# A decoder trunk on one core: the second head's flips moved behind the attention products, four loads given homes of their own or moved, and the bias copies cut in six

## The reference, cut to what matters

```python
# layer 0
rkv = einsum('cbsd,cde->cbse', x_mix[:3], w_rkv)          # receptance, key, value
w = -softplus(-(w0 + tanh(xw @ w1) @ w2)) - 0.5            # decay
a = sigmoid(a0 + (xa @ a1) @ a2)
g = sigmoid(xg @ g1) @ g2                                  # output gate
y = rwkv7_scan(r, decay, k, v, -kk, kk * a)                # 16 heads of 64
out = ((norm(y) + bonus) * g) @ w_o
# layer 1, 16 heads, three groups of (window, dilation)
q, k = rms_norm(q) * scale, rms_norm(k)
logits = q k^T + bias(table, distance)                     # banded
out_g, lse_g = softmax(logits) v, logsumexp(logits)
o = sum_g softmax_g(lse_g) * out_g;  x = x + o @ w_o
# each layer
x = x + (silu(gate) * up) @ w_out
```

## Time and profile before

| what | value |
|---|---|
| median of three runs | 1908.83 us |
| the profiled execution, its own time | 1911.89 us |
| its span, first to last instruction | 1910.1 us |
| mean granted clock of TensorE | 0.983 of full |
| PE busy | 1822.3 us, 95% |
| DVE, ACT, POOL busy | 916.8, 771.9, 194.0 us |
| chain that ended last | PE 67%, ACT 4%, issue 1%, DVE 1% |
| transfers | 155.01 MB, mean 81 GB/s |

### The profile page before, as it was taken

The page is one execution under the profiler, slowest core; times in us unless marked ns, Lnnn a source line. Parts: engine busy times, 40 slices in busy tenths (PEclk is TensorE's granted clock), DMA queues, the critical chain, the costliest instruction groups (busy, mean ns, idle before and its releaser), DMA issues.

```text
span 1910.1 us, 36221 instructions
## 1 busy us (share of the span) xinstructions
PE 1822.3 (95%) x15618; PEld 1382.3 (72%) x15618; DVE 916.8 (48%) x1561; ACT 771.9 (40%) x1310; POOL 194.0 (10%) x172
## 2 busy tenths in 40 slices
PE   8988999988999999999999999999999799999999
PEld 3745655555558888888887777777777688888887
DVE  6624555555444444433454654654654454444322
ACT  4333444443233222222456655655665532222211
POOL 0022333333000000000011111111111000000000
PEclk9988999998999999999999999999999899999999
DMA  3271011102013332333322222222222123333322
GB/s 115 84 249 47 28 31 30 31 28 83 28 55 111 94 98 95 100 99 100 99 78 78 78 67 80 81 63 87 78 67 67 45 90 100 98 100 100 99 93 95
DMA packets 57542, 155.01 MB, mean 81 GB/s; under 512 B 5591, under 2 KB 22535, under 8 KB 57384
## 3 DMA queue, kind: packets, MB, share of 16 engines
q1 hardware_dynamic: 57288, 152.63, 25.4%
q10 hardware_dynamic: 96, 0.07, 0.0%
HBM read 150.51 MB, written 11.61 MB: 85 GB/s over the span
## 4 chain that ended last, share of the span: by engine, by line
PE 67%; ACT 4%; issue 1%; DVE 1%; ACTq 0%; DVEq 0%
PE bank L520 65%; PE bank L523 2%; ACT f L1500 2%; ACT f L1513 1%; ACT f L1487 0%; ACT r L1478 0%; ACT f L1474 0%; DVE r L1861 0%; ACT f L1505 0%; DVE f L1584 0%; ACT r L1194 0%; DVE r L1573 0%; DVE f L1989 0%; ACT L1454 0%; DVE r L2006 0%
## 5 line engine op out<-in xcount | busy, mean ns | idle before, releaser
L520 PE MATMUL bank<-r 128*128 128x512 f32 x5424 | 1262.0, 392 | 6.9 <-DVE r L2006 3.7
L520 PEld LDWEIGHTS bank<-r 128*128 128x128 f32 x5424 | 1013.3, 188 | 234.6 <-issue 19.8
L520 PE MATMUL bank<-f 64*64 64x64 f32 (+5 forms) x9762 | 522.5, 260 | 56.9 <-ACT f L1266 15.6
L520 PEld LDWEIGHTS bank<-f 64*64 64x64 f32 (+3 forms) x9762 | 320.8, 144 | 245.9 <-issue 125.3
L1573 DVE TENSOR_TENSOR r<-f,r 128x1024 fp32r<-128x1024 f32 x222 | 273.2, 1231 | 385.3 <-ACT r L1194 385.3
L1194 ACT ACTIVATE r<-f 128x1024 fp32r<-128x1024 f32 x222 | 232.5, 1048 | 158.4 <-PE bank L520 141.2
L2158 POOL TENSOR_TENSOR r<-f,r 128x512 fp32r<-128x512 f32 x48 | 62.2, 1297 | 862.2 <-ACT r L1478 862.2
L1457 ACT ACTIVATE r<-f 128x512 fp32r<-128x512 f32 x44 | 27.8, 632 | 215.6 <-DVE f L1900 215.6
L1930 DVE TENSOR_TENSOR f<-bank,f 128x512 f32<-128x512 f32 x72 | 56.0, 778 | 87.7 <-PE bank L520 84.4
L1704 DVE TENSOR_TENSOR f<-bank,f 64x512 f32<-64x512 f32 x80 | 55.1, 689 | 65.7 <-PE bank L520 64.4
L523 PE MATMUL bank<-f 128*128 128x128 f32 x432 | 64.8, 280 | 20.8 <-ACT f L1513 14.2
(11 more groups left out here) (106 smaller groups left out, 927.8 us busy)
## 6 DMA issues: line engine op xcount, KB each, us to landing
f<-stream SPq DMA_DIRECT2D x245, 512.0 KB, 3.5
bias_copies<-bias_rows SPq DMA_DIRECT2D x3, 3072.0 KB, 24.4
f<-xT SPq DMA_DIRECT2D x16, 256.0 KB, 4.7
f<-lora_out SPq DMA_DIRECT2D x16, 128.0 KB, 3.8
f<-bias_copies SPq DMA_DIRECT2D x16, 128.0 KB, 3.2
f<-bias_copies SPq DMA_DIRECT2D x32, 64.0 KB, 3.0
outT<-f SPq DMA_DIRECT2D x8, 256.0 KB, 4.2
f<-wo_last SPq DMA_DIRECT2D x2, 512.0 KB, 6.0
```

The source lines that it names most:

```text
L520: return nc.tensor.matmul(out, lhsT, rhs, start=start, stop=stop, skip_group_check=True)
```

## The change

- Panel 11 (tile `PAN_WA`) goes to a home of its own, `O_TG`, and no longer through the raw buffer; SP issues it without a wait, and panel 13 waits only for the split of panel 9. `raw_in` counts the raw buffer's loads accordingly.
- At tile 11 ACT loads the sigmoid table set ahead of its wait, takes the Copy before the Tanh, and splits panel 13 after both.
- The gate and output-gate weights of pairs 0 and 1 get homes in the receptance mix's area and are loaded after tile 10, between panels 13 and 14.
- The three bias copies become six of half the size, one behind the panels of each of k = 0 to 5.
- In the attention stage PE's order in a slot becomes product, aux, first head's flip, logits or attend, second head's flip. ACT's becomes split, drain of head 0, aux, drain of head 1, squares; in slot 5 the split comes behind the drain of head 0.

```diff
@@ homes
-O_LWA = O_CM + N_CM
-O_LWG = O_LWA + 2 * 2 * P
-O_AR = O_LWG + 2 * 2 * P
+O_AR = O_CM + N_CM
...
-O_EP = O_CC + S
+O_LWA = O_CC + S
+O_LWG = O_LWA + 2 * 2 * P
+O_EP = O_LWG + 2 * 2 * P
+assert O_XM <= O_LWA and O_EP <= O_XM + KC * S
@@ 
+        def raw_in(eng, p):
+            early = p > PAN_WA and (p - PAN_WA) % RAW == 0
+            eng.wait_ge(s[f"w_raw{p % RAW}"], 16 * (p // RAW + 1 - early))
@@ SP
             def panel(p):
-                if p >= RAW and is_split(p - RAW):
-                    sp.wait_ge(s["w_lo"], split_of(p - RAW) + 1)
-                elif p >= RAW:
-                    sp.wait_ge(s["dense"], PANEL_AT[p - RAW])
+                held = p - RAW - (RAW if p - RAW == PAN_WA else 0)
+                if p == PAN_WA:
+                    sp.dma_start(f(O_TG, 1024), stream[p]).then_inc(s["w_wa"], 16)
+                    return
+                if held >= 0 and is_split(held):
+                    sp.wait_ge(s["w_lo"], split_of(held) + 1)
+                elif held >= 0:
+                    sp.wait_ge(s["dense"], PANEL_AT[held])
                 sp.dma_start(f(O_RAW + p % RAW * 1024, 1024), stream[p]).then_inc(...)
             for p in range(PAN_PROJ + RAW):
+                if p == PAN_PROJ:
+                    full(sp, PAN_WA - 1)
+                    for hp in range(2):
+                        gate_weights(hp)
+                        output_gate_weights(hp)
                 panel(p)
...
-            gate_weights(0) ... output_gate_weights(1)
-            sp.wait_ge(s["bias_dma"], 48)
-            for g in range(3):        # 16 rows each
-                sp.dma_start(copies ...).then_inc(s["bias_rep"], 16)
+            def copy_bias(n):         # 8 rows each
+                sp.dma_start(copies ...).then_inc(s["bias_rep"], 16)
             for k in range(-1, NHP - 1):
                 if k + 3 < NHP:
                     gate_weights(k + 3)
                 for p in (PAN_PROJ + 2 * (k + 2), PAN_PROJ + 2 * (k + 2) + 1):
                     if p < PAN_WO0 + RAW:
                         panel(p)
+                if 0 <= k < 6:
+                    if k == 0:
+                        sp.wait_ge(s["bias_dma"], 48)
+                    copy_bias(k)
@@ PE, decay_and_gate
-                pe.wait_ge(s[f"w_raw{t % RAW}"], 16 * (t // RAW + 1))
+                pe.wait_ge(s["w_wa"], 16)
-                    w = O_RAW + t % RAW * 1024 + c * P
+                    w = O_TG + c * P
@@ PE, attention
-                    if a >= 0 and 3 <= i <= 6:
-                        flip_probs(a, 0, i - 3)
                     if i and it < NHP:
                         projection_aux(it, i - 1)
...
                     if 3 <= i <= 6:
-                        flip_probs(a, 1, i - 3)
+                        flip_probs(a, 0, i - 3)
                     if i < 4:
                         logits(a, i)
                     if 4 <= i <= 7:
                         attend(a, i - 4)
+                    if 3 <= i <= 6:
+                        flip_probs(a, 1, i - 3)
@@ ACT, first stage
-                split_high(min(t + LEAD, PAN_PROJ - 1))
+                if t != PAN_WA:
+                    split_high(min(t + LEAD, PAN_PROJ - 1))
...
                 if t == PAN_WA:
+                    nc.scalar.preload_act_table_set("sigmoid_and_others")
                     full(act, t)
-                    A(f(O_TW, S, 0, LORA), banks[t % 2][0:LORA, :], ACT.Tanh)
-                    A(f(O_TA, S, LORA, P), banks[t % 2][LORA:P, :], ACT.Copy).then_inc(freed(t), 1)
+                    A(f(O_TA, S, LORA, P), banks[t % 2][LORA:P, :], ACT.Copy)
+                    A(f(O_TW, S, 0, LORA), banks[t % 2][0:LORA, :], ACT.Tanh).then_inc(freed(t), 1)
+                    split_high(PAN_PROJ - 1)
@@ ACT, attention
-                    if it < NHP:
+                    if it < NHP and i != 5:
                         split_high(p_of(T_QKV + 9 * it + i) + LEAD)
                     if a >= 0 and 3 <= i <= 6:
                         keep_flipped(a, 0, i - 3)
+                    if it < NHP and i == 5:
+                        split_high(p_of(T_QKV + 9 * it + i) + LEAD)
+                    if i and it < NHP:
+                        projection_aux(it, i - 1)
+                    if a >= 0 and 3 <= i <= 6:
                         keep_flipped(a, 1, i - 3)
                     if it < NHP:
-                        if i:
-                            projection_aux(it, i - 1)
                         squares(it, i)
```

More of the change, by code:

```diff
@@ L439, in panel @@
             def panel(p):
-                if p >= RAW and is_split(p - RAW):
-                    sp.wait_ge(s["w_lo"], split_of(p - RAW) + 1)
-                elif p >= RAW:
-                    sp.wait_ge(s["dense"], PANEL_AT[p - RAW])
-                sp.dma_start(f(O_RAW + p % RAW * 1024, 1024), stream[p]).then_inc(s[f"w_raw{p % RAW}"], 16)
[L446 to L454, removed]
+                held = p - RAW - (RAW if p - RAW == PAN_WA else 0)
[6 more added lines that the diff above has]
+                    sp.wait_ge(s["dense"], PANEL_AT[held])
+                sp.dma_start(f(O_RAW + p % RAW * 1024, 1024), stream[p]).then_inc(s[f"w_raw{p % RAW}"], 16)
             def gate_weights(hp):
@@ L466, in output_gate_weights @@
                              lora_out[:, 2:4, hp * P:(hp + 1) * P]).then_inc(s[f"lwg_in{hp % 2}"], 16)
[L468 to L471, removed]
-            sp.wait_ge(s["bias_dma"], 48)
-            for g in range(3):
[L474 to L477, removed]
+            for p in range(PAN_PROJ + RAW):
+                if p == PAN_PROJ:
[3 more added lines that the diff above has]
+                        output_gate_weights(hp)
+                panel(p)
+                if p == 1:
+                    sp.dma_start(f(O_OH, 3 * 384, 0, 33), const[0:33, C_OH:C_OH + 3 * 384]).then_inc(s["oh_in"], 16)
+                    sp.dma_start(f(O_REL, 48, 0, 33), rel33).then_inc(s["oh_in"], 16)
+                    sp.dma_start(con(C_ID), const[:, C_ID:C_ID + P]).then_inc(s["con_in"], 16)
+                    sp.dma_start(con(C_HEAD, 2 * P), const[:, C_HEAD:C_HEAD + 2 * P]).then_inc(s["con_in"], 16)
+            full(sp, T_WO0 - 1)
+            sp.dma_start(f(O_CM, N_CM), const[:, C_SCORE:C_OH]).then_inc(s["mask_in"], 16)
+            def copy_bias(n):
+                lo = n * 8 * 384
+                copies = bias_copies[lo * P:(lo + 8 * 384) * P]
+                sp.dma_start(copies.rearrange("(h i u) -> h i u", h=8, i=P),
+                             bass.AP(tensor=bias_rows.tensor, offset=lo, ap=[[384, 8], [0, P], [1, 384]]))\
                     .then_inc(s["bias_rep"], 16)
@@ L499, in _ @@
                     if hp == 0 and h == 0:
-                        sp.wait_ge(s["bias_rep"], 48)
+                        sp.wait_ge(s["bias_rep"], 96)
                         sp.wait_ge(s["hd_lo"], FC)
@@ L564, in plain @@
                     pe.wait_ge(freed(t), t // 2)
-                pe.wait_ge(s[f"w_raw{t % RAW}"], 16 * (t // RAW + 1))
+                raw_in(pe, t)
                 for c in range(KC):
@@ L605, in output_early @@
                     if col == 0:
-                        pe.wait_ge(s[f"w_raw{(PAN_WO0 + p) % RAW}"], 16 * ((PAN_WO0 + p) // RAW + 1))
+                        raw_in(pe, PAN_WO0 + p)
                     if c == 0 and m == 0:
@@ L628, in project @@
                 if c == 0:
-                    pe.wait_ge(s[f"w_raw{p % RAW}"], 16 * (p // RAW + 1))
+                    raw_in(pe, p)
                     if n:
@@ L1188, in split_high @@
                     p = panel_of(q)
-                    act.wait_ge(s[f"w_raw{p % RAW}"], 16 * (p // RAW + 1))
+                    raw_in(act, p)
                     if p == PAN_IN0 + 2:
```

## The result

The changed kernel takes 1873.51 us (median of 4 runs, 1873.18 to 1874.58), the kernel before 1908.95 (4 runs): 35.4 us less, a ratio of 0.9817, 95% interval 0.9801 to 0.9832. The forecast was 1880.5 us, 28.3 us less, with a range of 1875 to 1888. The profiled execution took 1873.18 us with a span of 1871.4.

What follows compares the result with a forecast made beforehand. PE, busy 95% of the span, bounds the kernel, so only its idle time or clock can give. 8.8 + 7.1 + 11.6 + 0.8 = 28.3 us off 1911.89 leaves 1883.6, as median 1880.5; own range 1876 to 1884.5, with rivals 1875 to 1888.

Steps and rivals of the forecast that it cites:

- Tile 11: End of first stage: PE's 1.50 us wait for the emptying of tile 11 goes, product 13 starting at 102.5; gain 1.5 us.
- Gate weights, clock and the chain over the masks: Scan start, k = -1: 4.35 us load wait and low clock go; first inverse at 121.6, 8.8 us earlier including tile 11.
- Bias copies: Scan, k = 0: the 5.73 us wait for panel 16 and low clock behind it go; 7.1 us, bounds 5.7 and 8.6.
- the three parts together: First-stage end and scan: tile 11, gate weights and bias copies, forecast as 8.8 + 7.1 us.
- Attention, seven iterations: Attention iterations with products: waits for the flips' drain go, 1.66 us each, 11.6 us in all; bounds 3.5 and 12.9.
- the residual wait of slot 5: Attention slot 5, second flip: 0 to 0.2 us of wait stays; 0.5 us or more would show the forecast wrong.
- The last iteration: Last attention iteration, without products: `attend` falls into a 1.85 us wait; 0.8 us off the end, bounds -0.6 and 1.9.
- the later exponentials: Last attention iteration: exponentials start about 0.5 us later, as slot 4's last drain stands behind `attend`.
- the lower clock did not return: Rival 3, attention: the clock falls once per iteration, seven times 1.62 us, 11.3 us, giving 1891.8; chance 0.04.
- rival 1: Attention slot 5: DVE or ACT limits the second flip, only the 0.25s go; 1 us times seven, 1887; chance 0.10.
- No copy held a panel: Rival 4, scan: bias copies hold a panel past its first use, up to 52 us lost, 1932; chance 0.02.
- the conversion to the median: Whole kernel: the profiled 1911.89 us lies 3.1 us above the runs' median, so 1883.6 becomes 1880.5.

Runs made afterwards that it cites:

- the second profile of the changed kernel: The changed kernel timed again with no edit: 1873.20 us, ratio 0.9815 to the kernel before; its profiled execution took 1875.32 us.

## Why the prediction was off

- **Tile 11** held in mechanism: no wait, product 13 in one run with 12. The 1.50 us were read off the matmul rows, and undoing it costs 1.8 us in the trace (2.8 of median): the same underestimate as in the attention part below, in small.
- **Gate weights, clock and the chain over the masks** held in mechanism: the first inverse is released by POOL, at full clock from 108 on. That it came at 121.77 against 121.6 is in part luck. 0.9 us of its 8.6 us came from ahead of tile 11, which began at 88.70 instead of 89.62; the profile before had lost 3.4 us of clock between 16 and 24 us, this one 1.7. Counted from the start of tile 11 the gain is 7.7 us, where 8.8 was forecast with a bound of 6.9. The forecast was too short in the chain from DVE L1662 (now L1685) to the end of `bt`: taken as the 8.98 us of before, it took 10.64 (110.98 to 121.62). DVE's scan took 1.63 us for 1.21, POOL's key scaling, now beside it, 2.04 for 1.26, and POOL's L2083 (now L2106) 1.50 for 1.06. What stretched them was not tested.
- **Bias copies** held in mechanism: no panel is waited for, and none of the six copies holds one. k = 0 ran at full clock after its 2.13 us wait, so it gave 8.5 us in this pair of profiles instead of 7.1, within the bounds; in the second profile of the changed kernel its first 174 instructions took 8.97 us instead of 7.42, which leaves 7.0. So 8.5 was the clock's luck. By the medians the three parts together gave 15.3 to 16.4 us for 15.9.
- **Attention, seven iterations**: this is the step that failed, "Per iteration 1.76 - 0.1 = 1.66, times seven 11.6 us; bounds 3.5 [...] and 12.9". Mechanism and order of events were right (no wait in slots 3, 4 and 6, slot 5 left with DVE's probabilities), the size was not: 2.48 us from one product to the same one an iteration later (70.82 to 68.34), 17.4 in seven. The wait was sized from the matmul rows, 1.76 us per iteration; the loads stood idle for 3.23 us in the same four slots, and 2.39 of them went. The upper bound rested on the same rows, so the range missed with it. The run with the old order in slots 3, 4 and 6 shows it apart from slot 5: these cost 1.4 us per iteration, where their matmul rows have 0.5. A second step failed too, with less weight: the residual wait of slot 5 was put at 0 to 0.2 us and is 0.62 (0.84 for the loads), which the prediction had named as a sign of being wrong (0.5 us or more). PE was ready 7.4 us behind the start of the slot's product and not 7.7, and DVE no sooner than before (7.9 us), since ACT did not reach the exponentials earlier as was expected: the first of them starts 2.0 us behind the same product, as before.
- **The last iteration** gave about 2 us for 0.8, just over its bound of 1.9. Slot 5's first flip in the timeline of 1440 to 1476:

```profile
1458.35 0.96 PE L540 MATMUL bank<-f 128*128 128x128 f32 x4 [4.18 <-DVE f L2012]
...
1460.71 1.12 PE L540 MATMUL bank<-f 128*128 128x128 f32 x4
...
1469.01 0.60 ACT L1570 ACTIVATE f<-bank 128x512 f32<-128x512 f32 x1 [1.23 <-PE bank L537]
```

 It is at 1458.35 against 1494.20, 35.9 us earlier, and ACT L1570, the Sigmoid at the end, is at 1469.01 against 1507.38, 38.4 earlier. Slot 3's first flip had come 36.2 us earlier (1449.13 for 1485.36), so the later exponentials cost 0.4 us, where 0.5 was forecast. The rest of the iteration gave 2.5 back: `attend` in a wait, and less time at the lower clock, a shortfall of 1.7 us against 3.4 from the start of the iteration to that Sigmoid.
- **Rivals.** In the seven attention iterations with products the lower clock did not return: no window of 1 us from 950 to 1457 is below 1.00, though each iteration has 42 transposes. By the Trainium skill ("TensorE: Matmul & The Clock Gate", Part 4: PE-mode transpose) the full clock does not engage for transposes; among products and `attend` the trace does not show a loss by them, in the order before or in this one. DVE became slot 5's limit, as rival 1 had it, but at 0.6 us and not at 1.3. No copy held a panel.
- **The profiled execution** lay 3.1 us over its median through its clock, and the conversion to the median took account of that rightly.

## What to carry to other kernels

Price a short wait between small PE operations by the idle time of the weight loads as well as by the gap between matmul rows, and check it against the starts of the operations around it. Here the loads' figure was twice the other and the right one, and moving independent PE work between two users of a single PSUM bank, with ACT's order to match, gave 19.4 to 20.4 us. Parts that open the same stretch need not add: undone one by one the three scan parts cost 19.5 us, together 15.3 to 16.4. For the bias copies the trace shows why (7.30 us of wait for 5.73); the rest of the difference is of the size of the spread. A table load behind a wait is idle time that one line moves; here it was worth 13 us, 9 as wait and the rest, as far as the traces show, by the clock.

## What the runs showed of the hardware

Two executions of one program lost different amounts of TensorE clock (32.4 and 27.3 us of shortfall over the whole span before; 15.4 and 18.8 after), at different places, and their times differed by nearly as much. After PE waits of 2.13 us the engine ran at the lower level (1.2 GHz) in some iterations and at 2.4 GHz in others of the same program; with waits of 0.85 us in their place it left 2.4 GHz only once in the loop, from 401 to 415 us, at the end of k = 5 and the head of k = 6, behind PE waits of 1.64, 1.47 and 0.80 us.
